# The sum of squares in two RMS norms: eight ones products, or VectorE additions and one ones product

## The reference, cut to what matters

```python
def rms_norm(x, g):
    xf = x.astype(jnp.float32)
    xf = xf * lax.rsqrt(jnp.mean(xf * xf, axis=-1, keepdims=True) + RMS_EPS)
    return (xf * g.astype(jnp.float32)).astype(x.dtype)
```

## Time and profile before

| | |
|---|---|
| median of three runs | 1528.91 us |
| the profiled execution's own time | 1524.33 us |
| its span, first to last instruction | 1522.5 us |
| TensorE (PE) busy | 96% of the span |
| VectorE (DVE), ScalarE (ACT), GpSimd (POOL) busy | 30%, 15%, 11% |
| mean granted TensorE clock | 0.985 |
| norm A in the span | about 208 to 226 us |
| norm B in the span | about 473 to 496 us |
| the experts (line 1609 on) | about 792 to 1512 us |

### The profile page before, as it was taken

One profiled execution on the slowest core, in us unless ns is written; L12 is line 12 of the kernel. 1 busy time (PEld: TensorE's weight loads), 2 busy tenths in 40 slices (PEclk: granted clock), 3 DMA queues, 4 the chain that ended last, 5 costly groups with the idle time before them and its releaser, 6 DMA issues.

```text
span 1522.5 us, 39202 instructions
## 1 busy us (share of the span) xinstructions
PE 1455.7 (96%) x17820; PEld 941.3 (62%) x17820; DVE 452.2 (30%) x976; ACT 223.4 (15%) x485; POOL 165.3 (11%) x208
## 2 busy tenths in 40 slices
PE   6999889999999999987989999999999999999996
PEld 4767777777777777777654545555454555545553
DVE  2399321111022756774431110212111021211123
ACT  3134220000001512333220000000000000000001
POOL 3227200000000325115200000000000000000100
PEclk9999999999999999998999999999999999999999
DMA  9637033434433430305579999999999999999995
GB/s 285 210 104 192 21 112 121 156 111 165 153 111 111 119 104 3 58 4 135 175 260 414 412 415 413 389 413 366 414 389 396 413 365 414 375 412 388 392 403 219
DMA packets 187551, 384.86 MB, mean 253 GB/s; under 512 B 42463, under 2 KB 125631, under 8 KB 187258
## 3 DMA queue, kind: packets, MB, share of 16 engines
q1 hardware_dynamic: 180352, 365.84, 65.3%
q0 software_dynamic: 3616, 12.85, 2.2%
q10 hardware_dynamic: 3418, 3.68, 0.7%
HBM read 375.59 MB, written 6.73 MB: 251 GB/s over the span
## 4 chain that ended last, share of the span: by engine, by line
PE 89%; DVE 6%; DMA 1%; issue 1%; ACT 1%; SPq 0%; POOL 0%; DVEq 0%; ACTq 0%
PE bk L1609 30%; PE bk L1626 15%; PE bk L1091 11%; PE bk L776 9%; PE bk L1104 6%; PE bk L1528 2%; PE bk L1575 2%; PE bk L1006 2%; PE bk L1197 1%; DMA ring<-in_w_in_even 1%; DVE left L2186 1%; DVE tops L2184 1%; PE bk L1119 1%; PE bk L1140 1%; PE bk L839 1%
## 5 line engine op out<-in xcount | busy, mean ns | idle before, releaser
L1609 PE MATMUL bk<-part,xe 128*32 128x352 f32 x6144 | 459.1, 460 | 2.3 <-DVE xe L2646 2.3
L1609 PEld LDWEIGHTS bk<-part,xe 128*32 128x32 f32 x6144 | 207.8, 110 | 248.2 <-issue 245.8
L1626 PE MATMUL bk<-part,hidT 128*32 128x256 f32 x4224 | 231.4, 379 | 1.2 <-DVE hidT L2685 1.2
L1626 PEld LDWEIGHTS bk<-part,hidT 128*32 128x32 f32 x4224 | 141.9, 110 | 88.6 <-issue 2.6
L2681 DVE TENSOR_TENSOR hp<-sg,bk 128x352 f32<-128x352 f32 x48 | 37.6, 782 | 468.7 <-PE bk L1609 468.7
L1091 PE MATMUL bk<-xn,ring 128*128 128x288 f32 x704 | 172.8, 409 | 3.2 <-DMA ring<-in_ffn_up 3.2
L1091 PEld LDWEIGHTS bk<-xn,ring 128*128 128x128 f32 x704 | 134.7, 191 | 41.0 <-issue 3.4
L776 PE MATMUL bk<-xg,ring 128*128 128x288 f32 x336 | 88.9, 425 | 8.6 <-DMA ring<-in_w_in_even 8.6
L776 PE MATMUL bk<-mx,ring 128*128 128x288 f32 x384 | 96.2, 409 | 0.0
L1104 PE MATMUL bk<-hid,ring 128*128 128x288 f32 x352 | 85.5, 406 | 0.0
L776 PEld LDWEIGHTS bk<-mx,ring 128*128 128x128 f32 x384 | 72.0, 190 | 20.4 <-issue 0.9
(11 more groups left out here) (528 smaller groups left out, 1307.8 us busy)
## 6 DMA issues: line engine op xcount, KB each, us to landing
part<-in_moe_gate SPq DMA_DIRECT2D x136, 704.0 KB, 7.5
part<-in_moe_up SPq DMA_DIRECT2D x136, 704.0 KB, 8.7
part<-in_moe_down SPq DMA_DIRECT2D x128, 704.0 KB, 8.6
ring<-in_rwkv_w_rkv SPq DMA_DIRECT2D x24, 512.0 KB, 4.1
ring<-in_ffn_gate SPq DMA_DIRECT2D x22, 512.0 KB, 5.5
ring<-in_ffn_up SPq DMA_DIRECT2D x22, 512.0 KB, 5.4
ring<-in_ffn_down SPq DMA_DIRECT2D x22, 512.0 KB, 4.3
ring<-in_w_in_even SPq DMA_DIRECT2D x16, 512.0 KB, 7.4
```

The lines of the kernel that those rows point to most:

```text
L1609: last = mm(banks[g][32 * c:32 * c + 32, 0:FQ], xe[:, k, 32 * g:32 * g + 32], parts[ph % 3][:, FH * k + FQ * c:FH * k + FQ * c + FQ], star ...
L1626: last = mm(down_bk[g // 2][32 * q:32 * q + 32, 256 * (g % 2):256 * (g % 2) + 256], hidT[:, half, g, 32 * m:32 * m + 32], parts[ph % 3][:, ...
```

## The change

VectorE adds the eight chunks of squares up in place, and TensorE then multiplies the one chunk that is left by the ones. At norm A that is three additions of 1152, 576 and 288 elements on each partition. At norm B chunks 0 to 3 are halved (576 elements) between the two halves of the down projection, and 576, 576 and 288 elements follow behind the gains of chunks 4 to 7. The finished chunk is told by one more step of `xn_ok`, so the later counts on it rise by one or two. The ones product is moved on TensorE behind f = 0, m = 1 at norm A, and behind early 2 at norm B.

```diff
-    def rms_pe(pe, n, square, bank=0):
-        for c in range(KC):
-            pe.wait_ge(sq_ok, KC * n + c + 1)
-            last = mm(bk[bank][:, 0:T], C["ones"], square[:, c], start=c == 0, stop=c == KC - 1)
-        last.then_inc(ssq_mm, 1)
+    def rms_pe(pe, n, square, bank):
+        pe.wait_ge(xn_ok, (n + 1) * (KC + 1))
+        mm(bk[bank][:, 0:T], C["ones"], square[:, 0], start=True, stop=True).then_inc(ssq_mm, 1)
...
-                    if f == 0 and m == 0:
+                    if f == 0 and m == 1:
                         rms_pe(pe, 0, sq1, 4)
...
-                pe.wait_ge(xn_ok, KC + k + 1)
+                pe.wait_ge(xn_ok, KC + 1 + k + 1)
...
         down_products(0, early)
         down_products(1, early)
+        down_products(2, early)
         rms_pe(pe, 1, sq2, 4)
-        down_products(2, early)
...
-            pe.wait_ge(xn_ok, 2 * KC + c + 1)
+            pe.wait_ge(xn_ok, 2 * KC + 2 + c + 1)
...
             V.tensor_scalar(xn1[:, c], xT[:, c], vecT[:, g_:g_ + 1], None, ALU.mult).then_inc(xn_ok, 1)
+        dve.wait_ge(sq_ok, KC)
+        link(V.tensor_tensor(sq1[:, 0:4], sq1[:, 0:4], sq1[:, 4:8], ALU.add))
+        link(V.tensor_tensor(sq1[:, 0:2], sq1[:, 0:2], sq1[:, 2:4], ALU.add))
+        V.tensor_tensor(sq1[:, 0], sq1[:, 0], sq1[:, 1], ALU.add).then_inc(xn_ok, 1)
         rms_factor(dve, link, 0, 4)
...
             if half == 0:
+                dve.wait_ge(sq_ok, KC + 4)
+                link(V.tensor_tensor(sq2[:, 0:2], sq2[:, 0:2], sq2[:, 2:4], ALU.add))
                 dve.wait_ge(out_done, 16 * OUT_0)
...
+        dve.wait_ge(sq_ok, 2 * KC)
+        link(V.tensor_tensor(sq2[:, 4:6], sq2[:, 4:6], sq2[:, 6:8], ALU.add))
+        link(V.tensor_tensor(sq2[:, 0:2], sq2[:, 0:2], sq2[:, 4:6], ALU.add))
+        V.tensor_tensor(sq2[:, 0], sq2[:, 0], sq2[:, 1], ALU.add).then_inc(xn_ok, 1)
         rms_factor(dve, link, 1, 4)
```

## The result

The changed kernel took 1521.01 us, the median of seven runs (1517.35 to 1523.85), against 1528.91 us before. The ratio is 0.9945, 95% interval 0.9933 to 0.9957: 8.4 us faster, between 6.6 and 10.2. Run again later beside the kernel before, it gave 0.9949 (0.9931 to 0.9967), 7.8 us. The forecast was 1522.1 us and -6.8 us.

A forecast was written before the change was run, and what follows sets the result against it. TensorE, busy 96% of the span, was taken as the bound. Norms A and B at -3.40 us each, clock at 0, gave -6.79 us: 1522.1 us from the median 1528.91, range 1517 to 1529 us.

The forecast's parts named there:

- What goes from TensorE, 7 x 0.485 us a norm: At norms A and B seven of eight ones products go: 3.40 us a norm, 6.79 us in all.
- The additions: On VectorE at both norms: 1.36, 0.76 and 0.45 us for 1152, 576 and 288 elements, plus 0.11 us per link.
- Covers: Additions end before TensorE's ones product: 6.7 us at norm A, 3.7 at B; `hid` has 3.3, set 2 1.8.
- The experts move with what stands ahead: In the experts, 830 to 1522 us, transfers are released by TensorE's progress, so their start moves with everything ahead.
- a start of the experts that has not moved by 6.8 us: At the experts' start: a sign that the forecast is wrong, if they do not start 6.8 us sooner.
- Rival 1: At norm B VectorE's chain becomes the bound of line 1140 and half is lost: 1525.5 us; chance 0.08.
- The clock, taken as 0 with -4 to +4 us: TensorE's lower-clock spells carried over unchanged, 0 us; bounds of two spells less or two more, -4 to +4 us.
- Rival 3: TensorE's clock deals anew with two lower spells gone, 4 us less: 1518 us; chance 0.11.
- Rival 2: Four more lower-clock spells, 8 us, between 640 and 792 us eat the gain: about 1529 to 1530 us; chance 0.13.
- Rival 4: State update, 640 to 690 us: 33 us run at the lower clock, 14 us lost, 1536 us; chance 0.06.

The follow-up runs named there:

- the parts: The changed kernel's norm A alone, then its norm B alone, the other norm keeping its eight products: 0.9979 and 0.9970 of the kernel before.
- The late sum: The changed kernel with twelve more linked additions of 576 elements ahead of norm B's last one: 0.9982 of the kernel before.
- the kernel with one ones product in the old places: The changed kernel with its ones product where the eight stood, ahead of up f = 0 and early 2: 0.9943, again 0.9954, of the kernel before.
- the doubled products: The kernel before with each norm's eight ones products made twice: 1.0065 of the kernel before, +9.9 us.
- full products: Time mix's 16-column and 16-row products widened to 128: changed kernel 0.9936, kernel before 0.9996, one ones product left in place 0.9930, all against the kernel before.

## Why the prediction was right

- **What goes from TensorE, 7 x 0.485 us a norm.** Right. Norm B delivered 3.40 us in the chain, norm A 2.45 us in the first profile and 3.40 us in the two profiles where the spell at 211 us had before's length. Timed, the parts are 3.2 and 4.6 us, together 7.8; the whole 8.4 and 7.8 us in two jobs. What was worked out, 3.4 us a norm and 6.8 us in all, lies in every one of these intervals, for the whole change in the first job at its small end (6.6 us).
- **The additions.** Right to 0.01 us each (1.36, 0.76 and 0.46 us against 1.36, 0.76 and 0.45); the link costs 0.03 us rather than the 0.11 allowed. Alone they cost nothing that can be measured.
- **Covers.** Right in size at both norms (set 2's 1.84 us, `hid`'s 3.3 us). The cover at the ones product of norm B was 3.96 us where I had 3.7.
- **The experts move with what stands ahead.** Right: their stretch kept its length, 730.7 us against 730.6. My sign "a start of the experts that has not moved by 6.8 us" did turn up in the profiled pair (4.12 us), and it was a bad sign: it took for granted that both executions have the same clock spells.
- **Rival 1.** It did not happen. Its price was worked out wrongly: I had the loss come out of VectorE's sets, after 3.7 us of cover and another 1.8. The late sum shows that TensorE itself stops at the ones product: everything beyond the first cover is paid in full, 5.6 us of a 9.5 us delay. The 1.8 us do not come on top.
- **The clock, taken as 0 with -4 to +4 us.** Needed as a range: in the profiled pair the spells gave 1.30 us ahead of norm A, and took back 0.95 us at norm A and 3.33 us behind the thin products, 3.0 us in all. That 0 was a good middle for the medians was luck, since no row of before spoke for it. My reason why spells could only lie between 640 and 792 us was wrong. I looked for idle time of TensorE, and the fall at 553 us came with TensorE busy 53.00 of the 53.00 us from 500 us on. The profile of before has lower-level spells outside that stretch too (mean clock 0.91 in 40 to 60 us, 0.83 in 80 to 100 us). The Trainium skill ("TensorE: Matmul & The Clock Gate", section "What's actually happening") has it that the point at which the clock rises isn't tied to the kernel's start. The traces agree: the spell at norm A was 3.4 us long in six profiles and about 6.8 us in eight, and the kernel with one ones product in the old places had it once at either length.
- **Rival 3** gave 1518 us; two of the seven executions lie there (1517.35 and 1518.12 us), the median does not. **Rival 2** gave 1529 to 1530 us, and no execution came near it: the slowest took 1523.85 us. **Rival 4** had 33 us at the lower level in 640 to 690 us. The mean clock there was 0.93 in place of 1.00, which is 7 us, because a spell of before at 689 us now began at 683; over 640 to 830 us it was 0.95 in both.

What stays open: whether norm B's 4.6 us hold more than the 3.4 us of its products, or only the noise of twelve runs. The same goes for the whole: the four timings of the changed kernel and of that with the old places give 8.4, 7.8, 8.7 and 7.0 us, all above 6.8, and the doubled products cost 9.9 us where 7.8 were worked out. Each interval holds the worked-out value, and the profiles show no other saving, but no experiment excludes a further 1 us or so, as from the clock.

## What to carry to other kernels

A reduction over chunks that a busy TensorE makes with ones products can be made first by an engine that is idle there; here it was worth the removed products in full, since the sum was ready when TensorE wanted the one product that is left. Work out that one cover, because beyond it the delay was paid in full here (5.6 us of a wait expected at 5.5). Leave the product where it stands if the cover holds there. And where a gain is under one per cent, don't read it off two profiles: here they showed 4.0 us of a gain of about 8.

## What the runs showed of the hardware

The granted clock can fall without any idle time of TensorE just ahead of it: at 553 us of the changed kernel's profile TensorE had been busy 53.00 of the 53.00 us since 500 us, and the clock fell inside products that read 16 of 128 rows. In four of the eight profiles that have this spell the fall lies inside those products, 2.0 to 2.4 us behind the start of the first, and in four within 1 us behind the last. Why it falls there no run shows; with full products the spell was gone and one at 670 to 680 us had come.

Between 40 and 830 us of the profiles the lower level comes in spells of about 3.4, 6.8 or 10.2 us.

The mean granted clock goes together with much of the scatter between executions. Over the 71 runs of the kernel before beside the experiments, it lay between 0.978 and 0.986, and span and clock had a correlation of -0.76 (-0.43, -0.75 and -0.91 in the three jobs by themselves): 1535.5 us was the median span at 0.979, 1527.4 at 0.984, 1524.8 at 0.986. A step of 0.001 of mean clock is 2 x 0.001 x 1528 = 3.1 us at the lower level, of which half, 1.5 us, would be lost with TensorE busy all the time, and the fitted line gives 1.3 us of span for it.
